# Transposed softmax probabilities handed over in two groups (eight key tiles, then the meta rows) in place of three, in a two-block transformer kernel

## The reference, cut to what matters

```
def gqa_block(q_blk, k, v):
    s = jnp.einsum('bkgqd,bksd->bkgqs', q_blk, k).astype(jnp.float32) * (HEAD_DIM ** -0.5)
    p = jax.nn.softmax(s, axis=-1)
    return jnp.einsum('bkgqs,bksd->bkgqd', p.astype(v.dtype), v)
...
a_out = attention_branch(q, k, v, q_norm_g[i], k_norm_g[i], cos, sin, n_tok) * jax.nn.silu(a_gate)
```

## Time and profile before

| | |
|---|---|
| median of 3 runs | 2446.06 us (2445.66 to 2452.49) |
| profiled execution, first to last instruction (span) | 2444.0 us |
| mean granted TensorE clock | 0.948 |
| PE busy | 2216.2 us, 91% |
| DVE busy | 1096.1 us, 45% |
| ACT busy | 802.1 us, 33% |
| POOL busy | 712.9 us, 29% |

### The profile page before, as it was taken

The page is one execution under the profiler, slowest core; times in us unless marked ns, Lnnn a source line. Parts: engine busy times, 40 slices in busy tenths (PEclk is TensorE's granted clock), DMA queues, the critical chain, the costliest instruction groups (busy, mean ns, idle before and its releaser), DMA issues.

```text
span 2444.0 us, 27898 instructions
## 1 busy us (share of the span) xinstructions
PE 2216.2 (91%) x10833; PEld 1829.6 (75%) x10833; DVE 1096.1 (45%) x1470; ACT 802.1 (33%) x1426; POOL 712.9 (29%) x548
## 2 busy tenths in 40 slices
PE   5989888999999966666999999997999999999996
PEld 4778668999777855556888888776888888878775
DVE  7245648898261088888222110336232323221433
ACT  5122217888141178885000000233122112111212
POOL 2312230000222322220233332223333333247762
PEclk8989999999999987777999999998999999999998
DMA  4122021010231100002111211233111111122332
GB/s 157 44 96 70 18 78 35 10 44 10 95 122 52 45 16 1 1 1 78 43 44 49 64 47 48 86 104 104 43 50 44 48 47 45 49 86 94 120 130 78
DMA packets 133594, 146.33 MB, mean 60 GB/s; under 512 B 5828, under 2 KB 105688, under 8 KB 133496
## 3 DMA queue, kind: packets, MB, share of 16 engines
q1 hardware_dynamic: 117655, 94.43, 12.7%
q10 hardware_dynamic: 15840, 50.54, 5.7%
HBM read 127.13 MB, written 17.83 MB: 59 GB/s over the span
## 4 chain that ended last, share of the span: by engine, by line
PE 55%; issue 24%; DVE 11%; ACT 4%; POOL 3%; DMA 2%; ACTq 1%; POOLq 0%; DVEq 0%
PE psum L469 18%; PE psum L470 18%; PE psum L471 18%; DVE softplus_part L1742 2%; POOL w_ring L403 2%; DVE softplus L1739 1%; DVE stick_w_t L1753 1%; DVE softplus L1744 1%; POOL w_ring L401 1%; PE psum L746 1%; DVE xn L1464 1%; ACT softplus_part L1226 0%; DMA w_staging<-in_w_out 0%; DVE h L1469 0%; ACT softplus_part L1222 0%
## 5 line engine op out<-in xcount | busy, mean ns | idle before, releaser
L400 POOL TENSOR_TENSOR w_ring<-w_staging,zero 128x8 fp32r<-128x8 f32 x174 | 42.1, 242 | 1523.3 <-PE psum L471 1504.8
L403 POOL TENSOR_TENSOR w_ring<-w_staging,w_ring 128x1024 fp32r<-128x1024 f32 (+1 forms) x174 | 435.5, 2503 | 14.5
L469 PE MATMUL psum<-ffn_in,w_ring 128*128 128x512 f32 x704 | 280.1, 398 | 11.1 <-DVE ffn_in L1469 11.1
L470 PE MATMUL psum<-ffn_in,w_ring 128*128 128x512 f32 x704 | 277.7, 395 | 0.0
L471 PE MATMUL psum<-ffn_in,w_ring 128*128 128x512 f32 x704 | 276.9, 393 | 0.0
L469 PE MATMUL psum<-h,w_ring 128*128 128x512 f32 x576 | 228.9, 397 | 4.8 <-DVE h L1469 3.4
L470 PE MATMUL psum<-h,w_ring 128*128 128x512 f32 x576 | 227.4, 395 | 0.0
L471 PE MATMUL psum<-h,w_ring 128*128 128x512 f32 x576 | 226.8, 394 | 0.0
L1875 DVE SCALAR_TENSOR_TENSOR up_buf<-psum,vectors,up_buf 128x1023 f32<-128x1023 f32 x44 | 56.4, 1283 | 309.4 <-ACT up_buf L1360 309.4
L401 POOL TENSOR_SCALAR w_ring<-w_staging 128x1016 fp32r<-128x1016 f32 (+1 forms) x174 | 185.1, 1064 | 0.0
L469 PEld LDWEIGHTS psum<-ffn_in,w_ring 128*128 128x128 f32 x704 | 132.6, 188 | 42.7 <-DVE ffn_in L1469 11.8
(11 more groups left out here) (266 smaller groups left out, 4920.8 us busy)
## 6 DMA issues: line engine op xcount, KB each, us to landing
w_staging<-in_w_in SPq DMA_DIRECT2D x58, 512.0 KB, 3.8
w_staging<-in_w_up SPq DMA_DIRECT2D x44, 512.0 KB, 3.8
w_staging<-in_w_down SPq DMA_DIRECT2D x44, 512.0 KB, 3.2
w_staging<-in_w_out SPq DMA_DIRECT2D x16, 512.0 KB, 3.8
x_again<-scratch_x ACTq DMA_DIRECT2D x16, 512.0 KB, 4.7
xin<-in_x ACTq DMA_DIRECT2D x8, 512.0 KB, 3.2
x_again<-in_x ACTq DMA_DIRECT2D x16, 256.0 KB, 2.7
scratch_x<-h ACTq DMA_DIRECT2D x8, 512.0 KB, 2.6
```

Of the source, the lines that this page charges most:

```text
L400: pool.tensor_tensor(WR[:, r, 0, w:width], WS[:, s, w:width], ZERO[:, :], ALU.add)
L403: pool.tensor_tensor(WR[:, r, 1, 0:width], WS[:, s, 0:width], plain(WR[:, r, 0, 0:width]), ALU.subtract).then_inc(S["w_split"], 1)
L469: pe.matmul(dst, sh, mh, start=first, stop=False)
L470: pe.matmul(dst, sh, ml, start=False, stop=False)
```

## The change

The two groups of four key tiles become one group of eight, which spans banks 3 and 4. PE still issues the same nine transposes in the same order into the same places; it raises `pt_mm` after the eighth and after the ninth. ACT and DVE take the eight tiles in one instruction each (128x1024 in place of two of 128x512), then, where they did before, the meta group. The counts of `pt_mm`, `pt_hi` and `pt_lo` go from three to two for a tile.

```diff
+        def turned_probs(x, g, t):
+
+            if g == 0:
+                return PT[:, x, 0:8, P * t:P * t + P], PB[:, 3:5, :].rearrange("p b (k n) -> p (b k) n", n=P)
+            return PT[0:META, x, 8, P * t:P * t + P], PB[0:META, 5, 0:P]
...
             def turn_probs(i):
                 pe.wait_ge(S["sc_exp"], 3 * i + 3)
-                for g in range(3):
+                for g in range(2):
                     if i:
-                        pe.wait_ge(S["pt_lo"], 3 * (i - 1) + g + 1)
-                    for kt in range(4 * g, min(4 * g + 4, KTILES)):
+                        pe.wait_ge(S["pt_lo"], 2 * (i - 1) + g + 1)
+                    for kt in range(8 * g, min(8 * g + 8, KTILES)):
                         first, rows = tokens_of(kt)
-                        ins = pe.transpose(PB[0:rows, 3 + g, P * (kt % 4):P * (kt % 4) + P],
+                        ins = pe.transpose(PB[0:rows, 3 + kt // 4, P * (kt % 4):P * (kt % 4) + P],
                                            PR[:, i % 2, first:first + rows], IDENT[:, :])
                     ins.then_inc(S["pt_mm"], 1)
...
                 if part == 0:
-                    pe.wait_ge(S["pt_lo"], 6 * (p + 1))
+                    pe.wait_ge(S["pt_lo"], 4 * (p + 1))
...
-            def probs_hi(i, groups=range(3)):
+            def probs_hi(i, groups=range(2)):
                 t = i % 4
                 if t % 2 == 0 and i >= 4:
                     act.wait_ge(S["av_mm"], i // 2 - 1)
                 for g in groups:
-                    n = 3 * i + g
-                    act.wait_ge(S["pt_mm"], n + 1)
-                    rows = P if g < 2 else META
-                    kts = slice(4 * g, min(4 * g + 4, KTILES))
-                    act.activation(PT[0:rows, 0, kts, P * t:P * t + P],
-                                   PB[0:rows, 3 + g, 0:P * (4 if g < 2 else 1)].rearrange("p (k n) -> p k n", n=P),
-                                   ACT.Copy).then_inc(S["pt_hi"], 1)
+                    act.wait_ge(S["pt_mm"], 2 * i + g + 1)
+                    act.activation(*turned_probs(0, g, t), ACT.Copy).then_inc(S["pt_hi"], 1)
...
-            def probs_lo(i, groups=range(3)):
+            def probs_lo(i, groups=range(2)):
                 t = i % 4
                 for g in groups:
-                    rows = P if g < 2 else META
-                    kts = slice(4 * g, min(4 * g + 4, KTILES))
-                    v.wait_ge(S["pt_hi"], 3 * i + g + 1)
-                    v.tensor_tensor(PT[0:rows, 1, kts, P * t:P * t + P],
-                                    PB[0:rows, 3 + g, 0:P * (4 if g < 2 else 1)].rearrange("p (k n) -> p k n", n=P),
-                                    plain(PT[0:rows, 0, kts, P * t:P * t + P]), ALU.subtract).then_inc(S["pt_lo"], 1)
+                    v.wait_ge(S["pt_hi"], 2 * i + g + 1)
+                    dst, src = turned_probs(1, g, t)
+                    v.tensor_tensor(dst, src, plain(turned_probs(0, g, t)[0]), ALU.subtract).then_inc(S["pt_lo"], 1)
```

More of the change, by code:

```diff
@@ L1123, in _ @@
                 if i:
-                    probs_hi(i - 1, range(2))
+                    probs_hi(i - 1, range(1))
                 act.wait_ge(S["sc_max"], i + 1)
@@ L1129, in _ @@
                 if i:
-                    probs_hi(i - 1, range(2, 3))
+                    probs_hi(i - 1, range(1, 2))
                 if i >= 5 and i % 2:
@@ L1680, in _ @@
                 if i:
-                    probs_lo(i - 1, range(2))
+                    probs_lo(i - 1, range(1))
                 if i >= 6 and i % 2 == 0:
@@ L1686, in _ @@
                 if i:
-                    probs_lo(i - 1, range(2, 3))
+                    probs_lo(i - 1, range(1, 2))
             probs_lo(HEADS * TT - 1)
```

## The result

| | before | changed |
|---|---|---|
| median | 2446.59 us (4 runs) | 2470.22 us (4 runs: 2467.56 to 2471.68) |
| profiled span | 2444.0 us | 2465.7 us |
| mean granted TensorE clock | 0.948 | 0.948 |

The ratio is 1.0092, with a 95% interval of 1.0077 to 1.0108: the changed kernel is slower by 0.9%. The forecast was 2468.0 us, and 2465.9 for the span. The medians differ by 23.6 us and the profiled spans by 21.7: each profiled execution was the fastest of its four, 2.7 us under the median for the changed kernel and 0.9 for the one before. What follows is read from the profiled executions.

What follows compares the result with a forecast made beforehand. The attention was taken as bound by a ring of transposes, ACT's copies, exponentials and scores, not PE's work. Terms 11.5 + 7.35 + 1.7 + 0.8 + 0.55 gave +21.9 us: 2468.0 us, range 2458 to 2477.

Steps and rivals of the forecast that it cites:

- a ring: Attention: transposes, ACT's high-part copies, exponentials, last scores, then the next transposes; 3.53 us bare, to grow by 0.37.
- short turns: Attention intervals between successive tiles' transposes with 12 attend matmuls; 31 of them, 3.52 to become 3.89 us, 11.5 in all.
- The release, +0.44: ACT's first copy waits for the eighth transpose instead of the fourth: four more at 0.109, +0.44 us a turn.
- The copy, -0.06: One 128x1024 ACT copy takes 0.91 us in place of 0.97 for two of 128x512: -0.06 a turn.
- The long turn, from 3.695 to 3.94: Attention turns with 15 attend matmuls: no longer set by PE's work; 30 of them, +0.245 us each, 7.35 in all.
- The 12 late turns, +1.7: Long turns whose exponentials miss overlapping the copy's end, laid to DVE's maximum's thin margin: 12 x 0.14 = 1.7 us.
- The ends, +0.55: Behind the last transposes, DVE's low parts end 0.55 us later, delaying the last attend matmuls and output projection.
- the exponentials did not wait for DVE: Rival: the later low part pushes DVE's maximum past the exponentials' start; 6.5 us on top, 2474.5; chance 0.15.
- PE's work hid nothing: Rival: PE's queue sets the attention's turns, so ACT's later release costs nothing; 2446, or up to 6 more; chance 0.08.
- Fewer instructions won: Rival: the deciding chain runs through high part, low part and maximum, saving 7.4 us; 2438.6; chance 0.04.
- The granted clock stayed at 1.00: Rival: PE idles more in the attention and its clock falls; 30 us for a few dips, 2498; chance 0.03.
- PE's digit: Profile sign: PE's busy share in the attention falls below 9 tenths or nearly, with waits for the exponentials.

Runs made afterwards that it cites:

- the release alone: Kernel before, only ACT's first high-part copy released later, by the sixth or eighth transpose instead of the fourth: ratio 1.0057 or 1.0106.
- DVE's part alone: Kernel before with one 128x1024 DVE low part in place of two of 128x512, ACT's two copies kept: ratio 1.0023.
- DVE in halves: Changed kernel with DVE's low part put back to two of 128x512, both behind ACT's one wide copy: ratio 1.0100.

## Why the prediction was right, point by point

**What bounds the attention.** Right: a ring through the transposes' release, ACT's copy, the exponentials and the scores, and not PE's work, though its busy share said so. Shown three ways: the release alone, at two sizes, moves the short turns in proportion; three matmuls less move nothing in the changed kernel; and the same three matmuls less bring the old long turn down to the ring's length and no further.

**The release, +0.44.** Measured +0.43: short turns of 3.526 became 3.957 with the release alone. One side remark of the working was off: what is left of 0.64 after three starts of 0.109 is 0.31 and not a transpose's 0.27. The term doesn't rest on it.

**The copy, -0.06.** Measured -0.058 a turn. The 128x1024 copy took 1027 ns on average, where 1025 was read from another line. By the Trainium skill's figures (ScalarE: Activation LUTs, What ACT_TABLE_LOAD costs) the estimate was 0.09; the runs don't agree with that, and do with the rows' 0.06.

**The long turn, from 3.695 to 3.94.** Measured 3.693 to 3.96, and 4.10 for the 12 late ones (4.08 forecast). The sum for the attention was 11.5 + 7.35 + 1.7 + 0.8 = 21.35, measured 22.0. The part mis-sized by most is the long turn, 0.02 each and 0.5 us in all: its ring before was 3.59, as the run with fewer matmuls showed, and not 3.57.

**The 12 late turns, +1.7.** The number was right and the reason wrong. The step "the margin stays thin, and I let the 12 turns lose 0.14 again" took DVE's maximum for the cause; they are tied to the partitions of an older pair's output. The trace of the kernel before could have told: its turn from 425.79 has the maximum's end 1.48 behind the transposes' start and is not late, and its turn from 454.74 has it at 1.45 and is.

**The ends, +0.55.** The part behind the last transposes grew by 0.5, but it varies by up to 4.8 us between kernels, so its length neither confirms nor denies the term. The rows do confirm it:

```profile
623.70 1.18 PE L664 MATMUL psum<-ident,probs 128*128 128x128 f32 x9 [0.64 <-ACT probs L1128]
...
625.86 1.41 DVE L1647 TENSOR_TENSOR probs_t<-psum,probs_t 128x1024 fp32r<-128x1024 f32 x2 [1.79 <-ACT probs_t L1098]
```

The low parts end 3.57 behind the last transposes' start, where they ended 3.04 behind it: +0.53.

**The total.** That the span came within 0.2 us of the forecast is in part luck. The attention grew by 0.65 us more than its sum, and the part ahead of it, for which the forecast has no term, was 0.8 us shorter, which is within what it varies by.

**The rivals.** In the changed kernel the exponentials did not wait for DVE: in the long turns the maximum ended at most 1.83 behind the transposes (1.79 was forecast), and at least 0.23 ahead of the exponentials. In the kernel with DVE's part alone they did wait, in 12 turns. PE's work hid nothing but the 0.09 of the long turns. Fewer instructions won 3.6 us on ACT and, by the run with DVE in halves, nothing on DVE. The granted clock stayed at 1.00 from 378 us to the last transposes, with 146 matmuls in 20 us as with 161.

**What the profile would show.** One mark was badly chosen: PE's digit was to fall below 9 tenths "or nearly", and it stayed at 19.88 of 20. The weight loads and the count of matmuls are what moved.

## What to carry to other kernels

Where two engines hand a piece of work to and fro, ask first for the length of the ring, not for busy shares: look for a turn in which the busiest engine had nothing extra to do, and compare its length with the ordinary one. If they agree, each 0.1 us of later release costs 0.1 us a turn, and merging instructions gains only what their overlap left, here 0.06 for one saved against 0.43 for the release given up. The Trainium skill (Perfetto Trace Analysis, Optimizing Scalar/DVE Operations) says that breaking up instructions on an engine which isn't saturated but causes bubbles elsewhere may let work be completed sooner. The trace agrees: with ACT's copy in two parts, the first released after the fourth transpose, the attention is 22.0 us shorter.

## What the runs showed of the hardware that was not expected

An ACT instruction of 128 partitions that would otherwise start about 0.11 before the end of the one ahead of it starts 0.02 behind that end in turns that follow a 64-partition ACT copy on partitions 64 to 127, and not where that copy works on partitions 0 to 63: 12 turns of 4.10 in place of 3.96, which move by a head when the halves are exchanged. What holds them up is open.

The 64-partition instructions themselves show the same. In the changed kernel ACT's rounding copy of the output (`mixed_a`) starts 0.09 ahead of the end of the meta group's copy where it works on partitions 0 to 63 (421.56 against 421.40 + 0.25), and 0.02 behind it on partitions 64 to 127 (437.38 against 437.11 + 0.25). DVE's first `attended` starts 0.09 ahead of the low part's end (421.38 against 420.24 + 1.23) or 0.04 behind it (429.35 against 428.09 + 1.22) in the same way; the instructions behind it lose about as much again, and DVE's next maximum is 0.24 later.

The part of the program ahead of the first and behind the last transposes, of which the edits touch at most the work on the last pairs, took 2216.0 us in the changed kernel (374.0 ahead and 1842.0 behind), 2216.4 in the kernel before, and up to 2222.7 (376.4 and 1846.3) in other kernels, there with three matmuls less in each of the last pairs. So a total of one execution can't tell 0.2% here, while the turns of kernels that should have equal ones agreed to 0.01 us.
